# A mixer and mixture-of-experts layer in split fp32: rows turned in place, operand addresses at one phase, weights loaded by quarters of rows

## Time and profile before

| | |
|---|---|
| median of 3 runs | 1679.69 us (1673.17 to 1682.93) |
| the profiled execution's own time | 1666.93 us |
| its span, first to last instruction | 1665.4 us |
| PE busy in the span | 1575.6 us (95%), 9060 matmuls |
| PE's weight loads | 1352.3 us (81%) |
| DVE, ACT, POOL busy | 1154.5, 663.0, 438.8 us |
| mean granted clock of PE | 0.975 |
| DMA of the span | 276.24 MB, mean 166 GB/s |

### The profile page before, as it was taken

How to read it: one execution, slowest core, us unless ns; L and a number is a source line. 1 busy time by engine, 2 the same in 40 slices (tenths; PEclk the granted TensorE clock), 3 DMA queues, 4 the chain that set the end, 5 groups by cost and what they waited for, 6 DMA issues and landing times. The chain is left out here.

```text
span 1665.4 us, 24090 instructions
## 1 busy us (share of the span) xinstructions
PE 1575.6 (95%) x9060; PEld 1352.3 (81%) x9060; DVE 1154.5 (69%) x1859; ACT 663.0 (40%) x904; POOL 438.8 (26%) x366
## 2 busy tenths in 40 slices
PE   8999999999999999999999729999999999999993
PEld 6788888888888888887888629989989898989893
DVE  4536867647867558585568676776778777878786
ACT  3224424143323143342243324544555454545552
POOL 2100006100035000062000044343445444444433
PEclk9999999999999999999999959999999999999997
DMA  7332345322435222534224535776777677867762
GB/s 243 130 98 77 109 145 183 121 76 85 169 127 178 77 77 101 173 131 152 77 77 147 209 100 169 236 221 201 250 244 254 218 258 235 273 213 263 236 206 98
DMA packets 96308, 276.24 MB, mean 166 GB/s; under 512 B 17168, under 2 KB 19344, under 8 KB 87488
## 3 DMA queue, kind: packets, MB, share of 16 engines
q1 hardware_dynamic: 67968, 187.63, 32.3%
q0 software_dynamic: 27648, 84.96, 17.3%
q10 hardware_dynamic: 576, 2.10, 0.3%
HBM read 229.66 MB, written 48.40 MB: 167 GB/s over the span
## 5 line engine op out<-in xcount | busy, mean ns | idle before, releaser
L1284 PE MATMUL mix_acc<-kept_xT,mix_w_high 128*128 128x512 f32 x640 | 259.2, 405 | 3.6 <-DVE mix_w_low L1093 3.0
L1286 PE MATMUL mix_acc<-kept_xT,mix_w_low 128*128 128x512 f32 x640 | 253.3, 396 | 0.0
L1285 PE MATMUL mix_acc<-kept_xT,mix_w_high 128*128 128x512 f32 x640 | 253.2, 396 | 0.0
L1675 POOL DMA_INDIRECT moe_x_quarter_rows<-x,kept_places x144 | 165.5, 1149 | 296.6 <-DVE moe_xT_first_tile L1972 154.3
L937 DVE TENSOR_TENSOR mix_w_low<-mix_w_raw,mix_w_high 128x2048 fp32r<-128x2048 f32 x71 | 163.3, 2300 | 112.4 <-ACT mix_w_high L750 112.3
L750 ACT ACTIVATE mix_w_high<-mix_w_raw 128x2048 fp32r<-128x2048 f32 x71 | 135.9, 1915 | 241.4 <-PE mix_acc L1286 241.4
L1940 DVE TENSOR_TENSOR moe_gate_up_low<-kept_w_gate_up_raw,moe_gate_up_high 128x2048 fp32r<-128x2048 f32 x64 | 146.6, 2290 | 50.0 <-ACT moe_gate_up_high L1796 50.0
L2338 PE MATMUL moe_gate_psum<-moe_xT_high,moe_gate_up_high 128*128 128x288 f32 x512 | 154.7, 302 | 20.4 <-DVE moe_xT_low L1980 20.4
L2340 PE MATMUL moe_gate_psum<-moe_xT_high,moe_gate_up_low 128*128 128x288 f32 x512 | 151.3, 296 | 0.0
L2339 PE MATMUL moe_gate_psum<-moe_xT_low,moe_gate_up_high 128*128 128x288 f32 x512 | 151.2, 295 | 0.0
L2338 PE MATMUL moe_up_psum<-moe_xT_high,moe_gate_up_high 128*128 128x288 f32 x512 | 151.1, 295 | 0.0
(11 more groups left out here) (476 smaller groups left out, 3479.8 us busy)
## 6 DMA issues: line engine op xcount, KB each, us to landing
mix_w_raw<-in_w_in SPq DMA_DIRECT2D x56, 1024.0 KB, 5.3
kept_w_gate_up_raw<-in_w_gate SPq DMA_DIRECT2D x32, 1024.0 KB, 7.0
kept_w_gate_up_raw<-in_w_up SPq DMA_DIRECT2D x32, 1024.0 KB, 12.3
queries_keys_or_down_raw<-in_w_down SPq DMA_DIRECT2D x32, 1024.0 KB, 11.3
mix_w_raw<-in_w_out SPq DMA_DIRECT2D x16, 1024.0 KB, 5.0
kept_conv_or_residual<-in_x POOLq DMA_DIRECT2D x16, 512.0 KB, 5.4
mix_x_rows<-in_x POOLq DMA_DIRECT2D x12, 512.0 KB, 4.5
x<-kept_conv_or_residual POOLq DMA_DIRECT2D x12, 512.0 KB, 2.9
```

Source lines behind the costliest of these rows:

```text
L1284: pe.matmul(out, ah, bh, start=first, stop=False)
L1285: pe.matmul(out, ah, bl, start=False, stop=False)
L1286: return pe.matmul(out, al, bh, start=False, stop=last)
L1675: pool.indirect_dma_start(out=X[:, m], out_offset=None, in_=x_quarters, in_offset=bass.IndirectOffsetOnAxis(ap=gather_i[:, at:at + 1], axi ...
```

## The change

Four things change together.
1. **The turn.** A block now takes 32 neighbouring columns of a quarter. The transpose reads and writes the same place in `X`, in one run of 1024 (A, B) or 256 (U) values. `XA` and `XT` are gone; `x_high` and `x_low` read `X`. The gather of the next rows waits for `x_low` of the same tile instead of its turn. The tiles are taken in the order U, A, B.
2. **The weights' rows.** Row 256j + 32b + d of w_gate and w_up now goes to partition 32j + d: eight DMAs of 0.5 MB, each into 32 partitions, in pieces of one row (2 KB).
3. **Addresses.** Chunks of `xTh`, `xTl`, `hTh` and `hTl` are 1280 bytes apart (5 x 256), and `columns` is 128 bytes longer, so that all that is declared after it starts at 192 past a multiple of 256, as `kept_xT` does.
4. **Orders.** DVE turns all tiles of e + 1 after `h_low` of f = 1; `row_norm` of the first tile stands after `h_low` of f = 0, that of the other after `h_low` of f = 3. ACT takes `x_high` of U ahead of `h_high` of f = 3, A and B behind it. POOL does all gathers, then `list_store`, then the three scatters. Ahead of the first expert, `rounds_needed` and `backs` come first, then turn and `x_low` tile by tile, and the turn of the second expert's A is no longer there.

```diff
@@ -1473,12 +1473,11 @@
...
-    half = keep.raw_gu.shape[2] // 2
+    quarter = w_gate.shape[0] // STRIPS
...
-        src = w.rearrange("(p c) n -> p c n", p=P)
-        for q in range(2):
-            c = slice(q * half, (q + 1) * half)
-            engine.dma_start(keep.raw_gu[:, k, c], src[:, c]).then_inc(keep.gu_in, 16)
+        for j in range(STRIPS):
+            rows = w[j * quarter:(j + 1) * quarter].rearrange("(b d) n -> d b n", d=TW)
+            engine.dma_start(keep.raw_gu[j * TW:(j + 1) * TW, k], rows).then_inc(keep.gu_in, 16)
@@ -1503,7 +1502,9 @@
...
+    STRIDE = CAP + UT
...
+    ORDER = (U, A, B)
@@ -1541,13 +1542,9 @@
...
-        XA = sb("xT_first_tile", [P, KC, P])
-        xTh = sb("xT_high", [P, KC, CAP], F32R)
-        with nc.sbuf_tensor("moe_xT_other_tiles", [P, KC, CAP], F32) as XT:
-            pass
-        xTl = sb("xT_low", [P, KC, CAP], F32R)
+        xTh, xTl = (sb(n, [P, KC, STRIDE], F32R) for n in ("xT_high", "xT_low"))
...
-        hTh, hTl = (sb(n, [P, FC, CAP], F32R) for n in ("hiddenT_high", "hiddenT_low"))
+        hTh, hTl = (sb(n, [P, FC, STRIDE], F32R) for n in ("hiddenT_high", "hiddenT_low"))
@@ -1620,6 +1617,15 @@
...
+        def turned_x(k):
+
+            m = BLOCKS[k]
+            return X[:, m[0]:m[-1] + 1].rearrange("p m (b i) -> p m b i", i=UT)
+
+        def low_rows(r, e, k):
+
+            return xl_done, r * (NE * COLS) + e * COLS + ORDER.index(k) + 1
+
@@ -1678,7 +1684,7 @@
...
-                    wait_apart(pool, idle, turned[k], r * NE + e + 1)
+                    wait_apart(pool, idle, *low_rows(r, e, k))
@@ -1722,7 +1728,7 @@
...
-                        wait_apart(pool, idle, turned[k], r * NE + NE)
+                        wait_apart(pool, idle, *low_rows(r, LAST, k))
@@ -1737,21 +1743,18 @@
...
-                for k in range(COLS):
+                for k in ORDER:
...
-                gather_next(r, 0, A)
-                gather_next(r, 0, B)
+                for k in ORDER:
+                    gather_next(r, 0, k)
...
-                gather_next(r, 0, U)
...
-                    gather_next(r, e + 1, A)
+                    for k in ORDER:
+                        gather_next(r, e + 1, k)
...
-                    gather_next(r, e + 1, B)
-                    scatter(r, e, A)
-                    gather_next(r, e + 1, U)
-                    scatter(r, e, B)
-                    scatter(r, e, U)
+                    for k in range(COLS):
+                        scatter(r, e, k)
@@ -1790,7 +1793,7 @@
...
-                act.wait_ge(gu_in, r * (NE * 64) + (e + 1) * 64)
+                act.wait_ge(gu_in, r * (NE * 128) + (e + 1) * 128)
@@ -1807,10 +1810,10 @@
...
-                if e and k == A:
+                if e and k == U:
...
-                src = XA[:] if k == A else XT[:, :, AT[k]]
-                act.activation(xTh[:, :, AT[k]], src, ACT.Copy).then_inc(xh_done, 1)
+                act.activation(xTh[:, :, AT[k]].rearrange("p b (m i) -> p m b i", i=UT), turned_x(k), ACT.Copy)\
+                   .then_inc(xh_done, 1)
@@ -1821,7 +1824,7 @@
...
-                act.activation(hTh[:, f], hT[:, f], ACT.Copy).then_inc(hh_done, 1)
+                act.activation(hTh[:, f, 0:CAP], hT[:, f], ACT.Copy).then_inc(hh_done, 1)
@@ -1915,10 +1918,10 @@
...
+                    x_high(r, e + 1, U)
+                    h_high(r, e, FC - 1)
...
-                    h_high(r, e, FC - 1)
...
-                    x_high(r, e + 1, U)
@@ -1963,21 +1966,15 @@
...
-                if e and k == A:
-                    wait_apart(dve, idle, xl_done, r * (NE * COLS) + (e - 1) * COLS + 1)
-                elif e:
-                    wait_apart(dve, idle, gu_used, r * (NE * FC) + e * FC)
-                rows = X[:, blocks[0]:blocks[-1] + 1].rearrange("p m (d b) -> p m b d", b=KC)
-                to = XA[:] if k == A else XT[:, :, AT[k]]
-                dve.transpose(to.rearrange("p b (m i) -> p m b i", i=UT), rows).then_inc(turned[k], 1)
+                rows = X[:, blocks[0]:blocks[-1] + 1].rearrange("p m n -> p (m n)")
+                dve.transpose(rows, rows).then_inc(turned[k], 1)
...
-                dve.wait_ge(xh_done, r * (NE * COLS) + e * COLS + k + 1)
-                sl = (slice(None), slice(None), AT[k])
-                src = XA[:] if k == A else XT[sl]
-                dve.tensor_tensor(xTl[sl], src, xTh[sl].bitcast(F32), ALU.subtract).then_inc(xl_done, 1)
+                dve.wait_ge(xh_done, low_rows(r, e, k)[1])
+                low, high = (a[:, :, AT[k]].rearrange("p b (m i) -> p m b i", i=UT) for a in (xTl, xTh))
+                dve.tensor_tensor(low, turned_x(k), high.bitcast(F32), ALU.subtract).then_inc(xl_done, 1)
@@ -1987,7 +1984,7 @@
...
-                dve.tensor_tensor(hTl[:, f], hT[:, f], hTh[:, f].bitcast(F32), ALU.subtract).then_inc(hl_done, 1)
+                dve.tensor_tensor(hTl[:, f, 0:CAP], hT[:, f], hTh[:, f, 0:CAP].bitcast(F32), ALU.subtract).then_inc(hl_done, 1)
@@ -2270,42 +2267,36 @@
...
-                turn(r, 0, A)
...
-                for k in range(1, COLS):
+                for k in ORDER:
...
-                for k in range(COLS):
...
-                turn(r, 1, A)
...
-                    if e == LAST:
-                        row_norm(r, LAST - 1, 0, 1)
...
+                    row_norm(r, e - 1, 0, 1)
...
+                    for k in ORDER:
+                        turn(r, e + 1, k)
...
-                    if e:
-                        turn(r, e + 1, A)
...
-                    row_norm(r, e - 1, 1 if e == LAST else 0)
...
-                    turn(r, e + 1, U)
...
-                    turn(r, e + 1, B)
-                    for k in range(COLS):
+                    row_norm(r, e - 1, 1)
+                    for k in ORDER:
@@ -2352,7 +2343,7 @@
...
-                                    xTh[:, c], xTl[:, c], c == 0, c == KC - 1)
+                                    xTh[:, c, 0:CAP], xTl[:, c, 0:CAP], c == 0, c == KC - 1)
@@ -2471,7 +2462,7 @@
...
-        columns = sb("columns", [P, 24])
+        columns = sb("columns", [P, 56])
```

## The result

The change makes the kernel slower: 1749.74 us median (1745.88 to 1752.09) against 1679.06 (a fourth run of the kernel before is in that median), a ratio of 1.042 (95% interval 1.039 to 1.046). The forecast was 1636, between 1617 and 1685. The profiled execution has a span of 1744.4 us. One execution of this document stands outside its ratio: of e6's four, one took 3197 us and the others 1737 to 1740.

A forecast was written before the change was run, and what follows sets the result against it. It took PE as the bound, through the distance between matmuls and PE's stops. Gains of 21.8 (phases), 20.5 (stop) and 2 us (start), 44.3 in all, took the median from 1679.69 to 1636, range 1617 to 1685.

The forecast's parts named there:

- Weights: Each expert's gate and up loads: 14 us and nothing, or twice 14, as bounds; no cost taken.
- Small pieces alone are no burden: Weight loads: w_in's 1 MB stages, also in rows of 512 values, land after 5.3 us.
- The four quarters ... can be under way together: Weight loads: quarter transfers in one queue, issued 0.4 us apart, can overlap; an argument against half-rate loading.
- Rival 1: Expert weights: quarter loads run at half the rate, 28 us instead of 14, and become the bound; 1769 us, chance 0.18.
- Phases: Mixer and expert matmuls: aligning operand addresses modulo 256 gains 21.8 us, bounds 8 and 26.
- Rival 2: Mixer and expert matmuls: address phase does not set their distance; only 22 us come, 1657 us, chance 0.12.
- Stop at chunk 3: Down products: PE's wait for h_low in nine experts goes through DVE's new order and faster turns; gain 20.5 of 21.7 us.
- The branch with turns at 2.2: DVE in the experts: turns at the old 2.2 us would leave 1.2 us of stop in each of nine experts.
- Start of the experts: Ahead of the first expert: PE starts at 991.4 instead of 993.45; gain 2 us, bounds 0 and 3.
- Gathers: POOL in the experts: gathers and the scatters behind them, 3 to 5 us later, stay hidden with 2 us to spare.
- rival 3: DVE in the experts: the stop moves instead of going, 12 to 15 us come back; 1649 us, chance 0.08.
- The sum: Whole kernel: 21.8 + 20.5 + 2 = 44.3 us gained, nothing paid; the median goes to 1635.4, said as 1636.

The follow-up runs named there:

- e6: Changed kernel with weights in 8 KB pieces, each transfer into 32 partitions, rows not matching x: ratio 1.042 against the kernel before.
- e5: Changed kernel with weights in 2 KB pieces, each transfer over all 128 partitions, rows not matching x: ratio 0.983 against the kernel before.
- e11: Changed kernel with the four quarter loads issued in one queue in the order 0, 2, 1, 3: ratio 1.039 against the kernel before.
- e1: Kernel before with only the quarter loads of the weights added: 1753.1 us, ratio 1.044.
- e2: Changed kernel with the loads of the kernel before (8 KB pieces, 128 partitions), rows not matching x: 1652.2 us, ratio 0.985.
- e7: Kernel before with the first row norm of a batch moved ahead of the hidden values of chunk 0 in every expert: ratio 0.987.
- e9: Kernel before with e7's norm place and 128 free bytes that put kept_xT at 64 past a multiple of 256: 1639.42 us, ratio 0.982.
- e8: e2 with POOL's stores of finished rows behind the three scatters: 1638.27 us, ratio 0.984 against the kernel before.
- e4: Changed kernel with the old loads and the matching in-place turn over columns 8 apart: 1682.53 us, ratio 1.003 against the kernel before.
- e14: e10 with e7's place of the first norm, before the hidden values of chunk 0: ratio 0.998 against the kernel before.
- e15: e14 with POOL's scatters ahead of the stores: ratio 0.993 against the kernel before.
- e10: Changed kernel with each weight's quarters from two queues, partitions 0 to 63 from SP and 64 to 127 from ACT: ratio 1.006 against the kernel before.
- e3: Changed kernel, same rows in the same places, but each transfer writes one 32-row block of all four quarters: 2201.57 us, ratio 1.312 against the kernel before.

## Why the prediction was wrong

**Weights: the step that failed.** It named the destination of 32 partitions as what has no row, bounded the load by 14 us and twice 14, and took "no cost". Measured, the quarter loads land 24.3 us behind their first issue on the mean (22.0 to 28.1), against 14.1 before, and PE waits ahead of fourteen of fifteen experts, all but the one behind the lists: 97 us. "Small pieces alone are no burden" was right (e5). "The four quarters ... can be under way together" was wrong for one queue: there even neighbours in different halves gained nothing (e11). That all 16 engines work on the same partitions then is the likely reading, and is not shown. The choice of the low end rested on rows of another width only. An unpriced term that is asked for once per expert, with a known break-even (1.55 times the present load) well inside its bounds, was worth more than 0.18.

**Rival 1 is what happened; that its time comes so near is in part luck.** It had 13.8 + 28 + 1.9 + 2.3 = 46.0 us per expert, and 2.5 us more in nine of them, 47.5 on the mean; measured is 46.5. Its load was 3 us too long (ACT reads 25.3 us behind the issue on the mean), and its issue too early: 16.7 us into the expert on the mean instead of 15.3, because DVE takes the statistics, 2.5 us, only behind the split that has waited for the load (in expert 5 from 1199.08). Its 1769 us lies 19 above the result. The estimate that the prediction worked out from the Trainium skill (SBUF — State Buffer, section "Door 1: The DMA port swizzle") lies 40 below, at 1710, and had the load right: 24 us. It holds the later issue of the nine experts (1636 + 15 x 3.5 + 22); missing are the 1 us between the last packet and ACT's read, the issue's other 1.4 us, and what the other terms gave too little. e1, e2, e5 and e6 show the rival by the time.

**Phases.** Right in kind, 21.8 against 16.7 in size. Mixer 15.3 against 10.3 (e7 to e9), and 11.5 in the change, where PE reaches its wait ahead of the experts at 980.09 - 18.54 = 961.55 instead of 993.45 - 20.36 = 973.09: records fall by 4 to 5 ns rather than 6. Gate, up and down 6.5 against 6.4: the undisturbed period goes from 38.65 to 38.25 (e8), 16 times 0.40. No run changes the stride alone, but the odd chunks show it: in the change chunks of either kind take 0.79 us.

```profile
1160.66 0.30 PE L2329 MATMUL moe_gate_psum<-moe_xT_high,moe_gate_up_high 128*128 128x288 f32 x1
...
1161.45 0.29 PE L2329 MATMUL moe_gate_psum<-moe_xT_high,moe_gate_up_high 128*128 128x288 f32 x1
...
1162.24 0.30 PE L2329 MATMUL moe_gate_psum<-moe_xT_high,moe_gate_up_high 128*128 128x288 f32 x1
```

Rival 2 is excluded for the mixer by e9, which moves one address; there the experts keep their stride and their 38.65 us.

**Stop at chunk 3.** Right: 20.5 forecast, 21 us by e7 (1.26% of 1669, with an interval of 17 to 25), by the norms' place alone. The turn in place takes 1202 ns where 1.2 was taken. The branch with turns at 2.2, "1.2 us of stop in each of the nine experts", is what e4 shows, 10.3 us in nine stops.

**Start of the experts.** Right: 2 us forecast, PE's wait falls from 20.36 to 18.54, 1.8 us. (The 1.05 and 1.18 us of `x_high` and `x_low` that it used are right, but do not stand in the rows that it names.)

**Gathers.** "Hidden, with 2 us to spare" failed. The scatters were put at T0' + 4 to 10; e2 has the first at 14.9, as the stores ahead of them (2.4 us each) were not counted and the gathers began only behind the list rows. This is rival 3's kind, a stop that moves. It shows in e2's rows and in e8's even distances, and in time only between e14 and e15. In e5 the waits stand behind the load instead: "14 us in all" left out that gathers beside it lengthen even the wide load. How the 18 us by which e2 misses the 44 forecast divide between the two is open.

**The sum.** What was right comes to 16.7 + 21 + 1.8 = 39.5 us, 2.4%. Without its quarter loads the change has 1.5 to 1.8% of it, with POOL's order as it stands (e2, e5) or with the scatters first (e8). Through the one failed term 1750 - (1679 - 26) = 97 us were lost.

## What to carry to other kernels

A load's cost is set by which partitions it reaches, not only by its bytes and pieces: before a layout is changed, ask how wide each transfer's destination is and what the outermost count of its source is. When a term has no row, hold its break-even point against its bounds; if it lies inside, it is a main case. And take apart changes of order: here one moved norm and 128 free bytes gave 1.8% (e9), as much as all other parts of the change do together without its loads (1.5 to 1.8%).

## What the runs showed of the hardware

- Transfers into 32 partitions, one behind the other in a queue, run at 195 to 210 GB/s with the DMA engines fully busy; two at once in different halves of the partitions run at 368 together (e10).
- POOL's gathers, scatters and list rows beside such a load of 4.19 MB lengthen it: 22.0 to 23.1 us with at most 0.5 MB of them, 24.7 to 28.1 with 1.7 to 2.3 MB (the change).
- Transfers whose source has an outermost count of 4 used 0.26 of the DMA engines' time, with fast packets (84 ns for 2 KB), and held SP for 1.4 us each (w_gate) and 3.6 us each (w_up) (e3).
- A mixer matmul whose operands both lie at 64 past a multiple of 256 takes 390 to 391 ns, and the same with both at 192 (the change); with one at 64 and one at 192 it takes 395 (e7, e9).
- DVE and ACT take 0.9 to 1.2 us more for 128 x 1024 values that they read 32 bytes apart (e4), and a transpose in place of neighbouring values takes 1202 ns, against 2211 for one of values 32 bytes apart.
